# Down projections of five FFNs: seven products of quarters in place of eight, with the sums made by GpSimd

## What is computed

```python
def swiglu(x, w_gate, w_up, w_down):
    return (jax.nn.silu(x @ w_gate) * (x @ w_up)) @ w_down     # F = 2816 hidden columns

h = h + 0.5 * swiglu(rms_norm(h, ffn_norm), w_gate, w_up, w_down)   # 4 times, 0.5
x = x + swiglu(rms_norm(x, ffn_norm), w_gate, w_up, w_down)         # 2 times, 1.0
```

## Time and profile before

| | |
|---|---|
| Median of three runs | 1742.52 us (1742.12 to 1743.49) |
| The profiled execution, its own time | 1742.88 us |
| Span of its trace | 1741.1 us |
| PE busy | 1728.5 us, 99% |
| DVE busy | 1262.9 us, 73% |
| ACT busy | 1002.9 us, 58% |
| POOL busy | 59.2 us, 3% |
| Chain of waits, share of PE | 91% |

### The profile page before, as it was taken

One profiled execution on the slowest core, in us unless ns is written; L12 is line 12 of the kernel. 1 busy time (PEld: TensorE's weight loads), 2 busy tenths in 40 slices (PEclk: granted clock), 3 DMA queues, 4 the chain that ended last, 5 costly groups with the idle time before them and its releaser, 6 DMA issues.

```text
span 1741.1 us, 24237 instructions
## 1 busy us (share of the span) xinstructions
PE 1728.5 (99%) x9535; PEld 1499.9 (86%) x9535; DVE 1262.9 (73%) x1602; ACT 1002.9 (58%) x1245; POOL 59.2 (3%) x95
## 2 busy tenths in 40 slices
PE   9999999999999999999999999999999999999998
PEld 8888998888888888888888888888888988888887
DVE  6766777766677666876667898867666898876665
ACT  6544657644467444754457866464446965565444
POOL 7200000000000000000001000000000000000000
PEclk9999999999999999999999999999999999999999
DMA  7755535665555655465645554356555554446552
GB/s 244 243 190 191 170 122 169 215 218 192 193 169 177 210 186 183 138 207 188 192 145 189 186 169 145 122 185 219 191 193 170 160 180 132 138 166 213 189 185 89
DMA packets 211564, 311.65 MB, mean 179 GB/s; under 512 B 6434, under 2 KB 166112, under 8 KB 211360
## 3 DMA queue, kind: packets, MB, share of 16 engines
q1 hardware_dynamic: 207472, 303.84, 53.1%
q0 software_dynamic: 3712, 6.44, 1.3%
q10 hardware_dynamic: 304, 0.33, 0.1%
HBM read 309.54 MB, written 1.05 MB: 178 GB/s over the span
## 4 chain that ended last, share of the span: by engine, by line
PE 91%; ACT 4%; DVE 3%; issue 1%; DMA 0%; SPq 0%; DVEq 0%; ACTq 0%
PE psD L1942 28%; PE psA L1831 27%; PE psA L1836 14%; PE psA L1909 3%; PE psA L1924 3%; PE psA L1775 3%; PE psA L1942 2%; PE psD L2228 2%; PE psA L1928 1%; PE psA L1913 1%; PE psA L1780 1%; PE psA L2012 1%; ACT hi L455 1%; PE psD L2165 1%; PE psD L2012 1%
## 5 line engine op out<-in xcount | busy, mean ns | idle before, releaser
L924 DVE TENSOR_TENSOR lo<-raw,hi 128x2048 fp32r<-128x2048 f32 x285 | 650.6, 2290 | 171.1 <-ACT hi L455 170.2
L455 ACT ACTIVATE hi<-raw 128x2048 fp32r<-128x2048 f32 x285 | 542.5, 1909 | 77.0 <-PE psD L1942 33.6
L1831 PE MATMUL psA<-xT,hi 128*128 128x512 f32 x2094 | 501.1, 390 | 0.1
L1831 PEld LDWEIGHTS psA<-xT,hi 128*128 128x128 f32 x2094 | 387.2, 188 | 76.9 <-DVE xT L957 0.3
L1836 PEld LDWEIGHTS psA<-xT,lo 128*128 128x128 f32 x2112 | 271.9, 191 | 11.8 <-issue 0.5
L1836 PE MATMUL psA<-xT,lo 128*128 128x256 f32 x2112 | 276.8, 283 | 0.1
L1942 PE MATMUL psD<-hi,prod_hi 128*128 128x512 f32 x544 | 173.6, 393 | 1.3 <-issue 1.3
L1942 PE MATMUL psD<-hi,prod_lo 128*128 128x512 f32 x544 | 171.9, 390 | 0.0
L1942 PE MATMUL psD<-lo,prod_hi 128*128 128x512 f32 x544 | 142.3, 389 | 0.0
L593 ACT ACTIVATE scr<-psA 128x512 f32<-128x512 f32 x66 | 39.4, 596 | 165.5 <-PE psA L1836 165.5
L608 ACT ACTIVATE prod_hi<-scr 128x512 fp32r<-128x512 f32 x66 | 41.7, 632 | 157.8 <-DVE scr L1306 157.8
(11 more groups left out here) (306 smaller groups left out, 1912.3 us busy)
## 6 DMA issues: line engine op xcount, KB each, us to landing
raw<-in_w_in SPq DMA_DIRECT2D x48, 1024.0 KB, 5.2
raw<-in_ffn_w_up SPq DMA_DIRECT2D x43, 1024.0 KB, 5.3
raw<-in_ffn_w_gate SPq DMA_DIRECT2D x43, 1024.0 KB, 5.4
raw<-in_ffn_w_down SPq DMA_DIRECT2D x43, 1024.0 KB, 4.9
raw<-in_w_gate SPq DMA_DIRECT2D x22, 1024.0 KB, 5.4
raw<-in_w_up SPq DMA_DIRECT2D x22, 1024.0 KB, 5.3
raw<-in_w_down SPq DMA_DIRECT2D x22, 1024.0 KB, 4.9
raw<-in_lru_w_in SPq DMA_DIRECT2D x10, 1024.0 KB, 5.3
```

The source lines that it names most:

```text
L455: act.activation(hi[:, n % RING, :], raw_of(n), ACT.Copy).then_inc(hi_ready, 1)
L924: dve.tensor_tensor(lo[:, n % RING, :], raw_of(n), hi[:, n % RING, :].bitcast(F32), ALU.subtract).then_inc(lo_ready, 1)
L1831: pe.matmul(psA[:, bank + f, :], w_hi[:, k, f * P:(f + 1) * P], xT[:, k].rearrange("p e s -> p (e s)"), start=(k == 0), stop=False)
```

## The change

In the FFNs numbered 1 to 5 (of 0 to 5) a run of q down blocks is computed another way, with q = 2, 2, 3, 4, 5. They are the blocks of chunks m+1 to m+q, with m = 8 - q, so the last of them belongs to chunk 8. Chunks 9 and 10 and chunks up to m keep the old form.

**Seven products.** With quarters x0..x3 and w0..w3 of the two matrices, the block is computed from seven products of sums of quarters:
- sums of x, in `tall`, seven tiles of 128 columns (896): the four quarters, two of them overwritten with sums, and three further sums;
- sums of w: w1 is overwritten with w1 - w0 (`first_sums`), and three new quarters are made (`other_sums`), in a buffer of 1536 columns (WIDE);
- four products are added over all q blocks in psA banks 0 to 3 (M1, M6, M7, M5), three go straight into psD banks 0 to 2 (C11, C12, C21). Seven products of three terms are 21 matmuls, not 24.

**Two units for one block.** In the sequence of weight blocks each of the q blocks becomes two units: one of 2048 columns (four products, 12 matmuls) and one of 1536 (three products, 9 matmuls). Both are split into `hi` and `lo`, and pass through the same ring of three. Their raw forms lie in `scr` (two or three buffers of 2048, two of 1536).

**Order.** The gates and ups of chunks m+1 to 9 come first, one after another without down blocks between them. Their products are kept in `tall`. Then come the 2q units, then the old down block of chunk m, then chunk 10 as before. The hardware loop has fewer turns (2, 2, 2, 1, 1) and more is written out.

**GpSimd** makes all sums: per block four of 512 columns for w and four of 128 columns for x, and per FFN four of 512 on the accumulators. The accumulators are copied from psA to `scr` by ACT (two copies of 1024 columns, `parts_out`) before the gates of chunk 10 may overwrite them, and DVE adds four results to h (`parts_added`, four operations of 512 columns), ahead of chunk 10's `gate_sum` in its list.

The core of the diff:

```diff
+WIDE, TALL = 3 * 512, 7 * P
+SEVEN = {1: 2, 2: 2, 3: 3, 4: 4, 5: 5}
+PAIR_LAST = CH - 3
...
@@ block.gpsimd
+                        def first_sums(k):
+                            w = view(raws[k % len(raws)], 4, 512)
+                            pool.wait_ge(seven_landed[k % len(raws)], 16 * seven_count[f, k])
+                            pool.tensor_tensor(w[:, 1, :], w[:, 1, :], w[:, 0, :], ALU.subtract).then_inc(first_sum, 1)
+                        def other_sums(k):
...
+                            if k >= len(wides):
+                                pool.wait_ge(lo_ready, n_seven + 2 * (k - len(wides)) + 2)
+                            pool_add(to[:, 0, :], w[:, 3, :], w[:, 1, :], ALU.subtract)
+                            pool.tensor_tensor(to[:, 1, :], to[:, 0, :], w[:, 0, :], ALU.subtract).then_inc(sums_ready, 1)
+                            pool.tensor_tensor(to[:, 2, :], w[:, 2, :], to[:, 0, :], ALU.subtract).then_inc(sums_ready, 1)
+                        def prod_sums(k):
+                            x = tall(f, k)[2].rearrange("p (m s) -> p m s", m=7)
+                            pool.wait_ge(seven_prod, seven_before[f] + k + 1)
+                            pool_add(x[:, 5, :], x[:, 0, :], x[:, 1, :], ALU.subtract)
+                            pool_add(x[:, 1, :], x[:, 1, :], x[:, 3, :], ALU.add)
+                            pool_add(x[:, 4, :], x[:, 1, :], x[:, 0, :], ALU.subtract)
+                            pool.tensor_tensor(x[:, 6, :], x[:, 2, :], x[:, 4, :], ALU.subtract).then_inc(seven_summed, 1)
+                        for k in range(q):
+                            if k < len(raws):
+                                first_sums(k)
+                            if k < len(wides):
+                                other_sums(k)
+                            prod_sums(k)
+                        for k in range(len(wides), q):
+                            if k >= len(raws):
+                                first_sums(k)
+                            other_sums(k)
...
@@ block.scalar
+                        for c in range(m + 1, CH - 1):
+                            split_to(n)
+                            gate_half(n + 1)
+                            n += 1
+                            split_to(n)
+                            silu(c0 + c, c)
+                            if c > m + 1:
+                                seven_high(c - m - 2)
+                            up_half(n + 1)
+                            n += 1
+                        for k in range(q):
+                            split_to(n)
+                            if k == 0:
+                                prod_high(p0 + m + 1, CH - 2, (m + 1) % 2)
+                            n += 1
+                            split_to(n)
+                            n += 1
+                        act.wait_ge(block_used, n)
+                        for e in range(2):
+                            act.activation(parts(f)[:, 2 * e:2 * e + 2, :], psA[:, 2 * e:2 * e + 2, :], ACT.Copy).then_inc(parts_out, 1)
...
@@ block.vector
+                        dve.tensor_tensor(x_lo, x, x_hi.bitcast(F32), ALU.subtract).then_inc(seven_lo, 1)
...
+                            step(dve.scalar_tensor_tensor(h[:, t, half_of[c]], parts(f)[:, at, :], col(FACTOR + t), h[:, t, half_of[c]], ALU.mult, ALU.add))
...
@@ block.tensor
+                        for to, x, w in products:
+                            own = to in (M1, M5, M6, M7)
+                            if own and k == 0:
+                                pe.wait_ge(up_summed if to in (M5, M7) else gate_summed, c0 + CH - 1)
+                            pe.matmul(bank(to), x_hi[:, x, :], w_hi[:, w, :], start=(own and k == 0), stop=False)
+                            pe.matmul(bank(to), x_lo[:, x, :], w_hi[:, w, :], start=False, stop=False)
+                        pe.wait_ge(lo_ready, n_at)
+                        for to, x, w in products:
+                            own = to in (M1, M5, M6, M7)
+                            last = pe.matmul(bank(to), x_hi[:, x, :], w_lo[:, w, :], start=False, stop=(own and k == q - 1))
...
+                        for k in range(q):
+                            seven(n + 1, n, k, ((M1, 0, 0), (C11, 2, 2), (C12, 6, 3), (M5, 1, 1)))
+                            seven(n + 2, n + 1, k, ((M6, 4, 0), (M7, 5, 1), (C21, 3, 2)))
+                            n += 2
+                        down(n + 1, n, p0 + m + 1, m)
```

More of the change, by code:

```diff
@@ L113, in build @@
         level_mask = sb("level_mask", [P, len(LEVELS), P], U8)
+        seven_x = {}
+        for f, q in SEVEN.items():
+            with ExitStack() as inner:
+                inner.enter_context(nc.sbuf_tensor(f"seven_gap{f}", [P, SEVEN_AT[f][0]], F32))
+                seven_x[f] = inner.enter_context(nc.sbuf_tensor(f"seven_x{f}", [P, 2 * TALL * q], F32R))
         scr = sb("scr", [P, SCRATCH])
@@ L431, in _ @@
         def _(act):
-            st = {"split": 0, "norm": 0, "updates": 0, "piece": 0, "ffn": 0, "step": 0, "rows": 0, "turned": 0, "gate": None, "gain": 0, "rstd": 0, "renorm": 0}
+            st = {"split": 0, "norm": 0, "updates": 0, "piece": 0, "ffn": 0, "prods": 0, "step": 0, "rows": 0, "turned": 0, "gate": None, "gain": 0, "rstd": 0, "renorm": 0}
             def step(ins):
@@ L910, in _ @@
         def _(dve):
-            st = {"split": 0, "norm": 0, "updates": 0, "piece": 0, "ffn": 0, "step": 0, "rows": 0, "update": None, "early": 2, "gain": 0, "rescaled": 0, "updated": 0, "renorm": 0, "between": None}
+            st = {"split": 0, "norm": 0, "updates": 0, "piece": 0, "ffn": 0, "prods": 0, "step": 0, "rows": 0, "update": None, "early": 2, "gain": 0, "rescaled": 0, "updated": 0, "renorm": 0, "between": None}
             def step(ins):
@@ L2128, in _ @@
                         pe.wait_ge(cpos_exp, 1)
-                    down(n + 5, n + 4, c0 + 1, 0, first=True)
+                    down(n + 5, n + 4, p0 + 1, 0, first=True)
                     n += 5
-                    with pe.Fori(0, (CH - 3) // 2) as j:
+                    with pe.Fori(0, J) as j:
                         for e in range(2):
```

310 lines of the change are left out of this document (264 added, 46 removed).

## The result

The median went from 1742.41 us (1742.12 to 1743.49) to 1765.03 us (1764.97 to 1765.99): ratio 1.013, 95% interval 1.0112 to 1.0148. The change costs 22.6 us. The forecast of slower was right; the number of 1754.0 (11.4 us more than before) has only half of the loss, and 1765 lies outside the range of 1735 to 1760.

The account below looks back on a forecast made before the run. PE, busy for 99% of the span, was taken as the bound. 48 fewer matmuls gave -10.9 us and losses in the units +22.3, so +11.4 on the median of 1742.52: 1754 us, range 1735 to 1760.

Parts of the forecast that it names:

- The exclusion in both directions: DVE operations with two SBUF inputs and GpSimd operations reading SBUF block each other; 22.3 us of losses, chance 0.56.
- With q = 5: Units of the five-block FFN: DVE's and POOL's times add up; 9.0 lost without gaps, 11.2 with turns, 10.2 taken.
- With q = 4: Units of the four-block FFN: DVE's and POOL's times add up; 4.7 us lost, 5.9 with turns, 5.3 taken.
- With q = 3: Units of the three-block FFN: 0.4 us lost, 4.6 with turns as DVE falls behind in earlier chunks; 2.6 taken.
- With q = 2: Units of both two-block FFNs: 0.6 us lost, 3.6 with DVE's arrears from the chunks before; 2.1 taken for each.
- The layout by turns: Upper end for the units: DVE and POOL each wait for the other's whole current operation; 11.2 us lost at q = 5.
- the gap-free sum: Lower end for the units: DVE's and POOL's times added with no gap allowed; 9.0 us lost at q = 5.
- The step that failed: Behind the units: accumulator copies, POOL's sums and DVE's additions end 12.7 us after them, covered by about 4 us; cost nothing.
- My rival of late accumulators: Behind the units: w_down's last block waits for chunk 10's product, 1 to 3 us in each FFN; no separate chance.
- The transitions without the port: Entering and inside the units, without DVE-GpSimd exclusion: PE waits for banks and ordered chains, 3.9 us for five FFNs.
- The rival of hidden additions: No exclusion, or DVE's slack pays for GpSimd's sums throughout: 7.0 us faster, 1735.5 us, chance 0.32.
- the signs announced: PE: 11 us less busy, some 20 idle; splits and sums up to 3.5; fourth-product wait at q = 2 showing arrears.

Follow-up runs that it names:

- run 2: The change with every GpSimd sum replaced by several fills that read nothing and together last as long or longer: 1743.46 us, ratio 1.0007.
- run 1: The change with every GpSimd sum replaced by one shorter fill that reads nothing: 1739.53 us, ratio 0.9987.
- run 3: The kernel before, with 60 GpSimd additions of 512 columns beside the last FFN, for which nobody waits: 1750.95 us, ratio 1.0047.
- run 4: The kernel before, with 120 GpSimd fills of 512 columns beside the last FFN: 1742.42 us, ratio 0.9999.
- run 13: The change with its block counts kept, each engine's list reordered inside and behind the units, sums still on GpSimd: 1753.88 us, ratio 1.0062.
- run 6: The change with only the four accumulator sums of each FFN replaced by equally long fills that read nothing: 1762.39 us, ratio 1.0113.
- run 8: The change with DVE's additions to h moved behind chunk 10's product in all five FFNs: 1763.65 us, ratio 1.0124.

## Why the prediction was off by half

**Right.** The exclusion in both directions, given 0.56, is what happened: the change against run 2 gives 21.6 us for the reading (against run 1, whose fills are shorter, 25.5), and runs 3 and 4 show the same in both directions without the change. The Trainium skill, "SBUF — State Buffer", section "Who interferes with whom", says that whichever of the two begins first blocks the other, and that a GpSimd instruction that only writes SBUF is no rival for VectorE's second input. The runs agree in both directions (splits up to 3.43 us, additions up to 3.36), and on the second point too: the fills of runs 2 and 4, which read nothing, left every split below 2.30.

**The units, term by term.** With q = 5: taken 10.2, between 9.0 and 11.2; measured 11.4. With q = 4: taken 5.3 (4.7 and 5.9), measured 5.7. With q = 3: taken 2.6 (0.4 and 4.6), measured 2.7. With q = 2: taken 2.1 twice (0.6 and 3.6), measured 1.6 twice. The sum is 23.1 for a forecast of 22.3. The layout by turns, each waiting for the other's current operation, was within 0.2 us at q = 4 and 5; the gap-free sum, 9.0 at q = 5, is about what a better order gets to in run 13 (9.5, a wait and half clock included). At q = 2 and 3 the layout by turns was too dark. But some of the 11.4 is no exclusion: up to 2 us are the granted clock at 0.50 (nine matmuls from 1723.47 to 1727.48, 4.0 us instead of 2.05), a term I did not have. That the layout came so near is in part luck.

**The step that failed** is "Cost nothing; that cover is about 4 us, since the product's chain behind the ups ends near 20", on the copies, POOL's sums and DVE's additions behind the units. Three things in it were wrong. First, the cover. By its own two numbers, 20 and 22, it was 2 us, not 4, and the kernel before had 2.1 us in FFNs 1 and 3, 1.6 in FFN 4, but 0.4 in FFN 5 and 0.2 in FFN 2, where PE wants the product after 18 matmuls and not after 24 (20.8 us after the units, not 22). Second, I applied the exclusion in the units and left it out of the sentence that costs GpSimd's sums behind them: the additions end 14.5 us after the units in FFN 3, not 12.7. Third, FFN 2 is not like the others: loads land late there (ACT waits 2.2 us for one), POOL has L479 right behind the sums, and DVE has `scale_pool`, which uses up the play that the chain has elsewhere. So `gate_sum` starts at 697.24, 1.20 us after PE's last two blocks begin at 696.04, where it started 4.73 ahead of them in the kernel before (689.96 and 694.69). It is 5.9 us late; less the slack of 0.2 this is the wait of 5.66. With the matmuls at half clock behind it this is 7.4 of the 10.3 us by which the FFNs' sum of 21.7 is above the forecast. The lists of DVE and PE in each FFN, or the 0.2 us between 698.56 and 698.80 in the kernel before, would have shown this before the fact. My rival of late accumulators had the mechanism, but at "1 to 3 us in each of five FFNs" and not as 7 in one.

**The clock.** In the change and in run 13, waits of 2.69 and 2.67 us were followed by 5 to 6 us at a granted clock of 0.50 (in runs 6 and 8 the same wait, 2.68 us, by 3 to 4). I had costed a wait at its own length. The 2.6 us of FFN 5 and some 1.7 of FFN 2 (7.4 less the wait of 5.66) come from that.

**What else.** 0.8 us more in FFN 1 I could not place. The transitions without the port were taken at 3.9 us, and the units of run 2 lost 4.9. Its FFNs' sum is +1.3, so 7.3 us more were lost outside the units (-10.9 + 4.9 + 7.3), 6.6 of them at FFN 2's end. In run 1 the units lost 4.6 and FFN 2's end 2.1. So the chain behind those units is a bound of its own, and only lengthened by the port. The rival of hidden additions (1735.5) had the same hole as the forecast: the least that a run without the sums' reading took is 1739.5 us, and with fills longer than the sums it was 1743.5.

**Of the signs announced**, new idle time before the units' matmuls, splits up to 3.4 us and sums up to 3.35 came, and the wait at the fourth product with q = 2 as well (0.99 us in FFN 1: the arrears, in small). PE's idle time rose by 19.5 us (from 12.6 to 32.1 of the span), where I had said some 20. But its busy time did not fall by 11 us: it rose by 2.5, since matmuls that stand alone are recorded with 0.39 to 0.50 us, not with their 0.228 us pace, and those at half clock with more.

## What to carry to other kernels

Where GpSimd reads SBUF beside VectorE operations with two SBUF inputs, add the times of both on one resource, in every stretch in which they meet, the small tail operations included; the busy shares of the whole span (77% and 17% here) say nothing of such a stretch. Then put the sums where VectorE has slack: here the loop took 45 additions for nothing, and three blocks at most, none in FFN 2, with the product ahead of the split turned a loss of 22.6 us into a gain of 3.2. When a change repeats in several stages, read the cover of each from the trace before, as the time from when the product is ready to when PE first takes it: the stage with an extra operation and an earlier want (here FFN 2) pays alone.

## What the runs showed of the hardware that I had not expected

- An operation of one column on DVE waits for a GpSimd addition: 1.28 us instead of 0.16 (run 3, L1005, both inputs in SBUF). In the same chain the operations with one input (L1000, L1003, of one column) never took over 0.17 us, but one of 18 multiplications of 128x128 with one tensor input (L1101) took 1.20 instead of 0.28. Why that one did, no run shows.
- Fills by GpSimd (0.53 us for 512 columns) disturb nothing, 120 of them in a row included.
- The granted clock fell to 0.50 around every wait of PE of 2.42 us or more in these runs (2.42, 2.63, 2.67 to 2.69, 3.69, 3.81 and on to 5.67). It stayed at 1.00 after those of 1.81 (the change, runs 1 and 6), but in run 8, where a wait of 1.79 ended at 1301.80, it was 1.00 until 1303.2 and 0.50 from 1303.6 to 1306.6. So the length of a wait alone does not decide it. The row is of run 1, after its wait of 1.81:

```profile
699.60:702.00 2.40, 2.33 (x10) 1.99 (x11) 2.12 (x1) 0.70 (x2) 0.00 (x0) 1.00 0.74 260
```
